# Two-layer block on one core: the second layer's last four weight units as sums of three rounded products, with the expert rooms asked for in another order

## The reference

```
u = rms_norm(x); q, k, v, hy, gts = split(u @ w_in)              # 10 weight units of 1024 x 512
attn  = diff_attention(q, k, v)        # 256 x 512, normalised per head of 128
hyena = hyena_mixer(hy)                # 256 x 512, long convolutions
g_attn, g_hyena = split(sigmoid(gts))  # 256 x 1024 each
merged = g_attn * (attn @ w_branch_attn) + g_hyena * (hyena @ w_branch_hyena)
x = x + merged @ w_out
x = x + expert_choice_ffn(rms_norm(x), w_router, w_gate, w_up, w_down)
```

## Time and profile before

| | us |
|---|---|
| median of 3 runs (1213.06, 1214.04, 1213.92) | 1213.92 |
| the profiled execution's own time | 1212.96 |
| its span, first to last instruction | 1210.9 |
| gate halves end, unit L2 + 10 starts on PE | 683.10 |
| first product with `w_out_2` | 713.45 |
| last route tile (L891) starts | 746.13 |
| first expert product starts | 763.68 |
| first refill of an expert room is issued | 772.21 |

### The profile page before, as it was taken

How to read it: one execution, slowest core, us unless ns; L and a number is a source line. 1 busy time by engine, 2 the same in 40 slices (tenths; PEclk the granted TensorE clock), 3 DMA queues, 4 the chain that set the end, 5 groups by cost and what they waited for, 6 DMA issues and landing times.

```text
span 1210.9 us, 16123 instructions
## 1 busy us (share of the span) xinstructions
PE 1112.0 (92%) x6491; PEld 786.3 (65%) x6491; DVE 501.3 (41%) x965; ACT 396.7 (33%) x760; POOL 16.3 (1%) x28
## 2 busy tenths in 40 slices
PE   6999999999999999899999996998978898879786
PEld 5778898886999999898678885433323232323231
DVE  4657775685666655576974523100100010001001
ACT  2432665934666544565345502000000000001000
POOL 3000000000000000000000000000000000000000
PEclk9999999999999999999999998899999999999999
DMA  7444543243344677444323695699999999999996
GB/s 227 159 148 151 177 140 139 88 141 138 140 170 177 164 183 192 155 140 148 131 70 131 250 384 207 259 430 427 430 426 430 426 430 426 429 428 429 427 422 254
DMA packets 94066, 309.42 MB, mean 256 GB/s; under 512 B 6000, under 2 KB 39032, under 8 KB 82040
## 3 DMA queue, kind: packets, MB, share of 16 engines
q1 hardware_dynamic: 93256, 307.42, 65.8%
q0 software_dynamic: 496, 1.07, 0.4%
q10 hardware_dynamic: 256, 0.10, 0.0%
HBM read 307.53 MB, written 1.05 MB: 255 GB/s over the span
## 4 chain that ended last, share of the span: by engine, by line
PE 72%; DMA 22%; DVE 3%; ACT 1%; issue 1%; SPq 0%; ACTq 0%; DVEq 0%
PE bank L435 71%; DMA parts_room<-in_w_up 7%; DMA arena<-in_w_down 3%; DMA arena<-in_w_up 3%; DMA parts_room<-in_w_down 3%; DMA ring<-in_w_down 3%; DMA xh<-in_w_down 2%; PE bank L644 0%; DVE roots_room L1597 0%; DMA arena<-in_x 0%; DVE parts L1625 0%; DVE arena L1560 0%; PE bank L548 0%; DVE hidden_parts L1833 0%; DVE arena L2150 0%
## 5 line engine op out<-in xcount | busy, mean ns | idle before, releaser
L435 PE MATMUL bank<-parts 128*128 128x256 f32 (+1 forms) x1872 | 242.5, 290 | 5.1 <-DVE parts L1639 4.3
L1625 DVE TENSOR_TENSOR parts<-ring,parts 128x512 fp32r<-128x512 f32 x288 | 193.2, 689 | 123.7 <-ACT parts L1224 122.4
L1224 ACT ACTIVATE parts<-ring 128x512 fp32r<-128x512 f32 x288 | 179.0, 628 | 198.8 <-PE bank L435 197.7
L435 PEld LDWEIGHTS bank<-parts 128*128 128x128 f32 x1872 | 232.4, 193 | 18.1 <-issue 14.8
L435 PE MATMUL bank<-hidden_parts,parts 128*128 128x256 f32 x1024 | 164.9, 283 | 0.0
L435 PE MATMUL bank<-arena 128*32 128x512 f32 (+5 forms) x516 | 148.6, 499 | 9.2 <-DMA arena<-in_w_down 2.7
L435 PE MATMUL bank<-arena,roots_room 128*32 128x512 f32 x400 | 131.5, 602 | 12.2 <-DMA ring<-in_w_gate 3.8
L435 PEld LDWEIGHTS bank<-hidden_parts,parts 128*128 128x128 f32 x1024 | 141.4, 192 | 0.1
L2137 DVE TENSOR_TENSOR sqr<-bank,arena 128x512 f32<-128x512 f32 x8 | 5.2, 685 | 269.8 <-ACT arena L1524 269.8
L435 PEld LDWEIGHTS bank<-arena 128*128 128x128 f32 (+3 forms) x516 | 74.6, 192 | 54.6 <-issue 43.3
L435 PE MATMUL bank<-ring,roots_room 128*32 128x512 f32 x224 | 95.3, 593 | 7.7 <-DMA xh<-in_w_up 3.9
(11 more groups left out here) (296 smaller groups left out, 1062.7 us busy)
## 6 DMA issues: line engine op xcount, KB each, us to landing
ring<-in_w_in SPq DMA_DIRECT2D x22, 2048.0 KB, 8.0
arena<-in_w_gate SPq DMA_DIRECT2D x14, 2048.0 KB, 34.8
arena<-in_w_down SPq DMA_DIRECT2D x13, 2048.0 KB, 37.3
arena<-in_w_up SPq DMA_DIRECT2D x11, 2048.0 KB, 36.8
ring<-in_w_ff_in SPq DMA_DIRECT2D x8, 2048.0 KB, 8.1
ring<-in_w_ff_out SPq DMA_DIRECT2D x8, 2048.0 KB, 9.0
parts_room<-in_w_up SPq DMA_DIRECT2D x8, 2048.0 KB, 36.8
ring<-in_w_gate SPq DMA_DIRECT2D x7, 2048.0 KB, 34.8
```

The lines of the kernel that those rows point to most:

```text
L435: return nc.tensor.matmul(o, lhsT=l, rhs=r, start=first, stop=last)
L1224: A(w_part[0][:, p % PIECES], piece_of(n, p), ACT.Copy).then_inc(S("pieces rounded"), 1)
L1625: X.tensor_tensor(w_part[1][:, p % PIECES], piece_of(n, p), w_part[0][:, p % PIECES].bitcast(F32), ALU.subtract).then_inc(S("pieces split" ...
```

## The change

- Units L2 + 10 to L2 + 13 are multiplied in rounded parts: 32 more pieces. `dense_split_short` does it for units 10 and 11, a written-out loop for 12 and 13. ACT and DVE get their rounding and subtracting; the inputs are rounded too (`hy_part`, `att_part`, and `merged2` into `h_part`, 16 blocks of 128 x 256 in all).
- Units 12 and 13 go through the two-slot ring. `merged2` takes the place of `gates_h`.
- `sub_stats` and `norm_heads` (the attention's norm per head) are done in three steps (heads 0 and 1; 2; 3) instead of two; the middle one moves into a = 6 and 7 of the loop.
- The copy of `xT` to `x2T` goes from POOL to ACT.
- ACT opens the two sets of gates at different places, with rounding between them.
- Four expert rooms are asked for between the last layer weights, and the ten rooms come in another order.

```diff
-        merged2 = area(0, 8, T)
...
+        merged2 = gates_h
+        att_part = [hidden_parts[:, i * 1024:(i + 1) * 1024].rearrange("p (k t) -> p k t", k=4) for i in range(2)]
+        hy_part = [hidden_parts[:, (i + 2) * 1024:(i + 3) * 1024].rearrange("p (k t) -> p k t", k=4) for i in range(2)]
...
-        moe_room = [cst[:, decay_end - UNIT:decay_end], area(19968, UNIT), area(12312, UNIT),
-                    ring[:, (L2 + 10) % RING, :], ring[:, (L2 + 11) % RING, :], xh.rearrange("p k t -> p (k t)"),
-                    parts_room[:, 0:UNIT], parts_room[:, UNIT:2 * UNIT], area(0, UNIT), area(8216, UNIT)]
+        moe_room = [area(19968, UNIT), cst[:, decay_end - UNIT:decay_end], area(12312, UNIT),
+                    xh.rearrange("p k t -> p (k t)"), area(0, UNIT), ring[:, (L2 + 12) % RING, :],
+                    ring[:, (L2 + 13) % RING, :], parts_room[:, 0:UNIT], parts_room[:, UNIT:2 * UNIT], area(8216, UNIT)]
...
+            def dense_split_short(n, h, src, entry):
+
+                ps = dense_bank((n, h))
+                for t in range(2):
+                    p = first_piece[(n, h // 2)] + 2 * (h % 2) + t
+                    pe.wait_ge(S("pieces split"), p + 1)
+                    for k in range(PIECE):
+                        if h == 0 and t == 0:
+                            pe.wait_ge(S("h split"), entry + k + 1)
+                        for m, (a, b) in enumerate(((0, 0), (0, 1), (1, 0))):
+                            last = mm(ps[:, t * T:t * T + T], w_part[a][:, p % PIECES, k, :], src[b][:, k, :],
+                                      k == 0 and m == 0, k == PIECE - 1 and m == 2)
+                    last.then_inc(S("pieces used"), 1)
...
-            pe.wait_ge(S("merged2"), 4)
...
+                    for q in range(KD // PIECE):
+                        p = first_piece[(n, h)] + 2 * t + q
+                        pe.wait_ge(S("pieces split"), p + 1)
+                        for k in range(PIECE):
+                            kk = PIECE * q + k
+                            if j == 0 and t == 0:
+                                pe.wait_ge(S("h split"), 6 * KD + kk + 1)
...
+            early = {L2 + 10: (0, 1), L2 + 12: (2,), L2 + 13: (3,)}
             for n in range(MOE):
+                for e in early.get(n, ()):
+                    load_expert(e)
...
+                if a == 5:
+                    for t in range(2):
+                        wait_taken(("hy time", 1, t))
+                    for k in range(4):
+                        A(hy_part[0][:, k, :], hyo[:, k, :], ACT.Copy).then_inc(S("h rounded"), 1)
+                round_half(LATE + 21 + a)
...
+                if a == 6:
+                    root_of(("sub", 1), T, "sub stats", 2)
...
+            open_gates(L2 + 8, gates_h)
+            root_of(("sub", 2), T, "sub stats", 3)
+            round_half(LATE + 29)
+            for k in range(4):
+                act.wait_ge(S("att normed"), (1, 1, 2, 3)[k])
+                A(att_part[0][:, k, :], att[:, k, :], ACT.Copy).then_inc(S("h rounded"), 1)
+            for h in range(2):
+                A(x2T[:, 4 * h:4 * h + 4, :], xT[:, 4 * h:4 * h + 4, :], ACT.Copy).then_inc(S("x2T copied"), 1)
+            round_half(LATE + 30)
+            open_gates(L2 + 6, gates_d)
+            round_half(LATE + 31)
...
+            rest_of_half(LATE + 29, 0, 2)
+            dve.wait_ge(S("gates opened"), 1)
+            open_hyena(0)
+            norm_heads(2)
+            rest_of_half(LATE + 29, 2, 4)
+            open_hyena(1)
+            for k in range(4):
+                rest_of(att_part, att, k, 5 * KD + 4)
...
-            pool.wait_ge(S(used_at[L2 + 11][0]), used_at[L2 + 11][1])
-            for h in range(2):
-                G.tensor_copy(x2T[:, 4 * h:4 * h + 4, :], xT[:, 4 * h:4 * h + 4, :]).then_inc(S("x2T copied"), 1)
-            pool.wait_ge(S("merged2"), 4)
+            pool.wait_ge(S("merged2"), 5)
```

More of the change, by code:

```diff
@@ L501, in token_split @@
                     dense_at[(n, t)] = ("pieces used", p + 1)
+                used_at[n] = ("pieces split", p + 1)
+            def dense_split_short(n, h, src, entry):
[10 more added lines that the diff above has]
+                    last.then_inc(S("pieces used"), 1)
+                dense_at[(n, h)] = ("pieces used", p + 1)
                 used_at[n] = ("pieces split", p + 1)
@@ L1082, in _ @@
                             .then_inc(S("lambdas loaded"), 16)
[L1083 to L1106 removed]
+            for n in range(4, GROUPS * MOE_UNITS):
+                load_expert(n)
             for h in range(2):
@@ L1488, in _, with round_merged @@
                 A(gates, gates, ACT.Sigmoid).then_inc(S("gates opened"), 1)
+            open_gates(L2 + 8, gates_h)
[9 more added lines that the diff above has]
+            round_half(LATE + 31)
+            def round_merged(k):
+                act.wait_ge(S("merged2"), k // 2 + 1 if k < 7 else 5)
+                A(h_part[0][:, k, :], merged2[:, k, :], ACT.Copy).then_inc(S("h rounded"), 1)
+            for k in range(4):
+                round_merged(k)
+            round_half(LATE + 32, 0, 2)
+            round_merged(4)
+            round_merged(5)
+            round_half(LATE + 32, 2, 4)
+            round_merged(6)
+            round_merged(7)
+            for m in range(33, 36):
+                round_half(LATE + m)
             for j in range(4):
@@ L1635, in rest_of_next, with rest_of @@
                     rest_of_piece(0, p, first, start)
+            def rest_of(part, src, k, entry):
+                dve.wait_ge(S("h rounded"), entry + k + 1)
+                X.tensor_tensor(part[1][:, k, :], src[:, k, :], part[0][:, k, :].bitcast(F32), ALU.subtract)\
+                    .then_inc(S("h split"), 1)
             def rest_of_h(src, h_set, k):
@@ L2041, in _, with add_attention @@
                                       ALU.mult), (n, h))
-            dve.wait_ge(S("gates opened"), 2)
-            for h in range(4):
+            def add_attention(h):
                 n = L2 + 11
```

171 lines of the change are left out of this document (103 added, 68 removed).

## The result

The changed kernel is slower, by 0.27%. Its median is 1215.63 us (1213.12 to 1219.5, 20 runs), that of the kernel before in the same session 1213.0 (1210.67 to 1215.09, 20 runs); the ratio is 1.0027 [1.0017, 1.0036]. I had forecast 2.2 us less and got 2.6 more, outside my range.

The account below looks back on a forecast made before the run. PE's chain up to the first refill was taken as the bound, then the DMA-limited expert stream. Terms -9.1 - 0.4 + 2.3 + 2.4 + 2.3 + 0.3 = -2.2 us gave 1211.7 us, range 1207.6 to 1214.8.

Parts of the forecast that it names:

- What bounds the kernel: PE's path before the route tiles sets the first refill; the end follows 438.7 us later; earlier expert loads gain nothing.
- my sign for a harmful order of the rooms: Behind the first refill: a time to the end other than 438.7 us would mean the room order matters.
- Products: Units 10 to 13: 32 pieces at 1.44 us take 46.1 us instead of 55.2, -9.1 us.
- steps 1 and 2: Added ACT and DVE work delays PE: +2.3 us in the loop before att2_out(3), +2.4 us in the branch products.
- the price of a piece: Rounded products of units 10 to 13: 1.44 us per piece of 12 products while PE is the limit.
- the 0.3 us at the first piece of unit 11: Branch products: a further PE wait of 0.3 us there, counted within the +2.4 us.
- the 0.4 of the statistics: Middle and last norm statistics cost one product each instead of two behind the loop, -0.4 us.
- Step 3: Merging: PE waits 4.2 us for merged2's forming, rounding and rests, against 1.9 before, +2.3 us.
- the sign: Between 690 and 718 us PE waits on DVE three or four times, 6 to 7 us in all.
- Step 4: Mixing: ACT and DVE keep up, also around the route tiles; only the last sum with x costs more, +0.3 us.
- Rival 2: Merging: the clock dips once, about 3.2 us at half speed lose 1.6 us; 1213.3 us, no visible change; 14%.
- The fourth rival: Mixing, pieces 48 to 63, at 1.2 GHz: 10 to 11 us low cost +3, 1217 us, slower; 13%.

Follow-up runs that it names:

- e12: Kernel before the change plus 21 constant products in TensorE's idle times between route tile 3 and the first expert product; 1209.11 us, ratio 0.9969.
- e4: Changed kernel with all ten expert loads queued behind the last layer weights, room order kept; 1216.12 us, ratio 1.0028.
- e1: Changed kernel with keep_tokens(0) on DVE moved behind the last piece's rest and the third sum with x; 1212.82 us, ratio 0.9997.
- e9: Changed kernel with ACT's squares of route tile 0 moved ahead of rounding the last four pieces, DVE's order kept; 1212.45 us, ratio 0.9993.
- e10: e6 with keep_tokens(0) put back where the changed kernel has it, ahead of the last rests; 1212.64 us, ratio 1.0001.
- e2: Changed kernel plus 3 and 4 constant products, results unread, in PE's two waits of the merging; 1215.39 us, ratio 1.002.
- e6: Changed kernel with units 10 and 11 back to plain fp32, keep_tokens(0) as in e1, middle root ahead of the sigmoids; 1205.19 us, ratio 0.9942.
- e3: Changed kernel with both edits, that of e1 and that of e2; 1208.82 us, ratio 0.9973.
- e5: Changed kernel with units 12 and 13 back to plain fp32 from the ring, merged2 not rounded; 1213.62 us, ratio 1.001.
- e11: e5 plus four constant products in the one wait of the merging; 1210.89 us, ratio 0.9989.
- e7: e3 plus 21 constant products in TensorE's idle times between route tile 3 and the first expert product; 1208.23 us, ratio 0.997.
- e8: e6 plus 21 constant products in TensorE's idle times of the routing; 1206.2 us, ratio 0.9953.

## Why the prediction was wrong

**What bounds the kernel: right in the main.** The refill and the time moved together in all runs but e12 (table), and the expert loads' early requests were worth nothing that shows (e4). But I had let everything behind route tile 3 move with it unchanged, and the way from the first expert product to the refill took from 7.1 to 9.2 us. And my sign for a harmful order of the rooms, a time behind the refill other than 438.7 us, proved nothing: it was 440.1 in the changed kernel and 438.75 in e1, with the same order of rooms.

**Products, steps 1 and 2: right but for 0.5 us.** From the issue of unit 10's load, `att2_out(3)` starts after 24.8 us, as forecast. The branch products wait 0.93 and 1.06 where I had 1.0 and 1.1. Unit 11 ends after 52.05 instead of 51.5. What was off is the price of a piece: ten pieces without a wait took 14.85 us, 1.49 each and not 1.44, and the other six were dearer too, while the 0.3 us at the first piece of unit 11 did not come. So the 4.6 us that rounded parts should save in units 10 and 11, and the 0.4 of the statistics, are spent but for a tenth: 2.3 before `att2_out(3)` (24.8 us after the issue against 22.5 before), 2.0 in these two waits, and about 0.7 on the dearer pieces.

**Step 3, merging: right, a little less.** 0.22 + 1.30 + 2.04 = 3.6 us of waiting, for a forecast 4.2. With the branches' two that makes 5.6 us, where I had named 6 to 7 as the sign.

**Step 4, mixing: this failed.** I wrote that "ACT and DVE keep up, also around the route tiles". Their rates do; their order does not. I had laid out three queues, but for `keep_tokens(0)` I let DVE wait only for PE's route tile. I left out that it also waits for ACT's squares, and that these stand in ACT's queue behind four pieces which need PE's progress. That is +2.86 us. e1 and e9 took it away from either side, e10 put it back.

**Rival 2, the dip in the merging, came true** (I had given it 14%). It cost 1.5 us, for a forecast 1.6. I had treated it as a choice between outcomes. It is a cost added to the forecast. e2 and e10 also show a dip behind the 2.86 us wait when none came before it.

Sum for the stretch to route tile 3: forecast -2.2, first half +0.5, merging -0.6, wait +2.9, dip +1.5, the remainder +0.1, which makes +2.2 us, as measured (88.76 against 86.52). With 0.4 at the start of the expert stream the whole way is 2.6 us longer, 0.22%, and the ratio says 0.27.

The fourth rival, the mixing at the lower clock throughout, gave nearly the right time for the wrong reason: by the two windows above, (1 - 0.95) x 2 x 4 + (1 - 0.63) x 2 x 4 = 3.4 us were low.

**What the change could have given.** The two halves of it are worth very different things. Rounded parts in the mixing give 0.58% by themselves (e6). In the branch products they give nothing, and they cost the mixing: with unit 11 in parts the waits of the merging are 3.6 us instead of 0.57. DVE's rests of unit 11 stand in its way there, but e6 takes away ACT's roundings of that unit too and moves a root, so the runs don't part the three. The difference is that of e3 and e6, 108.7 us of whole way against 105.4.

## What to carry to other kernels

When work is added to in-order engines, list for every wait in the stretch all the engines that it waits for, and what stands ahead of the signal on each. A wait that was harmless becomes part of a loop (PE waits for DVE, DVE for ACT, ACT for PE's progress) as soon as paced work is put ahead of the signal: nothing stops for good, but PE stands until the signal has gone all the way round. Judge a faster form stage by stage: the same form gained 5.7 us (4.6 in products, 1.1 in a shorter wait) where ACT and DVE had time for it, and nothing where they had sigmoids, roots and reciprocals to do as well. From 686 to 713 us of the changed kernel they were busy for 21.0 and 20.2 of 27 us, and PE still waited for them: the order of their work counted, and not only its amount. And take away TensorE's waits together, since removing one of two gaps may only move the clock's fall to the other.

## What the runs showed of the hardware

- No length of one gap alone tells in these runs whether the clock falls. Behind gaps of 1.3 and 2.0 us with 0.94 us of work between them it fell to 1.2 GHz in the changed kernel and cost 1.5 us (8.32 against 6.83 us for the same 54 records); the later gap of 2.86 us then brought no fall (24 records in 3.11). With the first two filled, the gap of 2.86 did bring one (4.59), and in e4 both did. A gap of 1.70 us left the clock alone in the kernel before, one of 1.89 let it fall in e5. In e12 it fell (0.63 from 760 to 764 us) with no gap of over 0.63 us in the 12 us before.
- The Trainium skill, TensorE: Matmul & The Clock Gate, The HAM clock gate, says that the gate's count runs freely and does not start with the kernel, so that the same work can meet it at another phase. The pair before and e5, and the pair after and e4, agree with that without proving it.
- Products that compute nothing, put into the gaps of the merging, kept the clock up behind them in e2, e3 and e11 at no measurable cost: the 54 records start 58.17 us after the issue of unit 10's load in e2, 58.20 in the changed kernel. In the idle times of the routing they kept it up in e7 and e8 and not in e12.
- The gather's 16 products took 3.97 us at 2.4 GHz (e7) and 3.97 us nearly all at 1.2 (e3), with 3.81 us of weight loads in both, while the expert products behind them went from 0.85 (the kernel before) to 0.44 us apart (e12).
